# Expert products with the tokens stationary and 512 weight columns (256 gate, 256 up) moving

## What is computed

```python
gate, idx = lax.top_k(aff.T, cap)              # cap = 128 for each expert and group
xe = jnp.take(tok, idx, axis=0)
h = jax.nn.silu(jnp.einsum('ecd,edf->ecf', xe, w_gate)) * jnp.einsum('ecd,edf->ecf', xe, w_up)
ye = jnp.einsum('ecf,efd->ecd', h, w_down) * gate[..., None].astype(x.dtype)
out = jnp.zeros_like(tok).at[idx.reshape(-1)].add(ye.reshape(-1, D))
```

## Time and profile before

| | us |
|---|---|
| Time, median of 3 runs | 3319.93 (3319.58 to 3321.43) |
| Span of the profiled execution, first to last instruction | 3317.6 |
| TensorE busy | 3111.9 (94%) |
| VectorE busy | 1891.1 (57%) |
| ScalarE busy | 1357.6 (41%) |
| GpSimd busy | 477.4 (14%) |

### The profile page before, as it was taken

One profiled execution on the slowest core, in us unless ns is written; L12 is line 12 of the kernel. 1 busy time (PEld: TensorE's weight loads), 2 busy tenths in 40 slices (PEclk: granted clock), 3 DMA queues, 4 the chain that ended last, 5 costly groups with the idle time before them and its releaser, 6 DMA issues.

```text
span 3317.6 us, 54591 instructions
## 1 busy us (share of the span) xinstructions
PE 3111.9 (94%) x21544; PEld 2878.0 (87%) x21544; DVE 1891.1 (57%) x2257; ACT 1357.6 (41%) x1668; POOL 477.4 (14%) x387
## 2 busy tenths in 40 slices
PE   7998999989958999999999999999999999999990
PEld 7997888968848998998989989899898999989990
DVE  6545777856664555555545555555555555555546
ACT  3216777861113334333334343333434333343423
POOL 2543232401120000010010000100010010110005
PEclk9999999999979999999999999999999999999995
DMA  6331101013344566565565655656566565665535
GB/s 203 124 100 49 33 9 30 33 62 121 116 165 133 201 200 204 191 191 202 193 206 190 199 191 191 206 200 197 191 197 203 195 191 198 202 193 202 180 126 215
DMA packets 367271, 533.68 MB, mean 161 GB/s; under 512 B 32592, under 2 KB 307792, under 8 KB 367056
## 3 DMA queue, kind: packets, MB, share of 16 engines
q1 hardware_dynamic: 352464, 488.48, 43.8%
q0 software_dynamic: 10368, 37.75, 4.4%
q10 hardware_dynamic: 4224, 4.19, 0.4%
HBM read 469.57 MB, written 60.82 MB: 160 GB/s over the span
## 4 chain that ended last, share of the span: by engine, by line
issue 66%; PE 18%; DMA 5%; POOLq 4%; POOL 3%; DVE 2%; DVEq 1%; ACT 1%; SPq 0%; ACTq 0%
PE ps_o L747 5%; DMA acc_d<-ysb,idx_s 4%; PE ps_pv L683 4%; PE ps_t L672 3%; PE ps_s L637 2%; PE ps_s L638 2%; POOLq L1585 1%; PE ps_l L764 1%; POOLq L1462 1%; POOLq L1470 1%; POOL qkv L1476 1%; PE ps_m L692 1%; POOLq L1576 1%; POOL w_l L1568 1%; PE ps_m L623 1%
## 5 line engine op out<-in xcount | busy, mean ns | idle before, releaser
L838 PE MATMUL ps_gu<-x_h,w_h 128*128 128x256 f32 x4096 | 1160.5, 283 | 20.0 <-issue 18.5
L838 PE MATMUL ps_gu<-x_h,w_l 128*128 128x256 f32 x4096 | 1159.1, 283 | 0.0
L838 PE MATMUL ps_gu<-x_l,w_h 128*128 128x256 f32 x4096 | 1159.1, 283 | 0.0
L1338 DVE TENSOR_TENSOR w_l<-w_raw,w_h 128x2048 fp32r<-128x2048 f32 x380 | 859.4, 2290 | 288.0 <-ACT w_h L1076 288.0
L838 PEld LDWEIGHTS ps_gu<-x_h,w_h 128*128 128x128 f32 x4096 | 786.3, 192 | 25.8 <-issue 23.9
L1076 ACT ACTIVATE w_h<-w_raw 128x2048 fp32r<-128x2048 f32 x384 | 719.3, 1907 | 195.5 <-PE ps_y L853 186.3
L838 PEld LDWEIGHTS ps_gu<-x_l,w_h 128*128 128x128 f32 x4096 | 786.3, 192 | 0.1
L838 PEld LDWEIGHTS ps_gu<-x_h,w_l 128*128 128x128 f32 x4096 | 786.3, 192 | 0.0
L1101 ACT ACTIVATE sg<-ps_gu 128x256 f32<-128x256 f32 x256 | 98.1, 383 | 941.9 <-PE ps_gu L838 941.9
L1389 DVE TENSOR_TENSOR hf<-sg,ps_gu 128x256 f32<-128x256 f32 x256 | 107.1, 418 | 578.4 <-ACT sg L1101 578.4
L853 PE MATMUL ps_y<-w_h,hh 128*128 128x512 f32 x1024 | 321.5, 395 | 0.0
(11 more groups left out here) (193 smaller groups left out, 3909.6 us busy)
## 6 DMA issues: line engine op xcount, KB each, us to landing
w_raw<-in_w_gate SPq DMA_DIRECT2D x128, 1024.0 KB, 5.3
w_raw<-in_w_up SPq DMA_DIRECT2D x128, 1024.0 KB, 6.1
w_raw<-in_w_down SPq DMA_DIRECT2D x128, 1024.0 KB, 6.0
xin<-in_x SPq DMA_DIRECT2D x16, 512.0 KB, 5.9
xln_d<-xln SPq DMA_DIRECT2D x16, 512.0 KB, 5.5
res<-xln_d SPq DMA_DIRECT2D x16, 512.0 KB, 3.2
h_d<-hid SPq DMA_DIRECT2D x16, 512.0 KB, 2.6
acc_d<-acc SPq DMA_DIRECT2D x16, 512.0 KB, 2.6
```

Of the source, the lines that this page charges most:

```text
L838: last = nc.tensor.matmul(ps_gu[n % 3][:, u, :], w[:, k, cols], a[:, k, :], start=k == 0 and q == 0, stop=k == KD - 1 and q == 2)
L1338: nc.vector.tensor_tensor(w_l[:, c % RING, :], w_raw[:, c % RING, :], w_h[:, c % RING, :].bitcast(f32), ALU.subtract).then_inc(w_lo, 1)
```

## The change

The tokens of one group (128) become the stationary operand of the gate and up products, and the weights move, 512 columns at a time: 256 of gate and the same 256 of up, side by side.

- There are 8 blocks j of 256 hidden columns (`FBLK`). A weight piece is now half of the contraction (4 steps, `KC`) with gate and up columns beside each other, loaded by two DMAs. `landed` gives the count for both.
- A block is two halves, `gate_up(e, j, 0)` and `gate_up(e, j, 1)`; each has 12 products for token group 0 and 12 for group 1. Each group has a bank of its own, `ps_gu[n % 3]` with n = 2j + g. TensorE signals the end of the first half (its weight piece is free) and, in the second half, of each group.
- ScalarE's silu and VectorE's product work on 128 tokens by 256 hidden columns of a group. `hf` now has tokens on the partitions, so TensorE transposes it, four tiles of 128x128 a block, into `ps_x` (`hidden_transposes`): for block j - 1 between the halves of block j, for the last block after down step 0.
- ScalarE copies the four transposed tiles to `hh` in one instruction (`hidden_hi`), VectorE writes `hl` in one (`hidden_lo`) and signals `h_split`.
- ScalarE and VectorE take one weight piece, then the transposed tiles of the block before, then the two groups, then another weight piece. The first x round waits until the transposed tiles have been read out of `ps_x`.

```diff
         def used(e, c):
             if c < NUP:
-                return gu_done, KF * e + 2 * (c // 2) + 2
+                return gu_done, GU * e + 3 * (c // 2) + (3 if c % 2 else 1)
             return dn_done, (KF // 2) * e + (c - NUP) + 1
+
+        def landed(e, c):
+            return W_ROUND * e + 16 * (2 * (c // RING) + 2 if c < NUP else 2 * (NUP // RING) + (c - NUP) // RING + 1)
...
# SyncE
                     if c < NUP:
-                        w = (w_gate, w_up)[c % 2]
-                        src = w[ex, :, (c // 2) * 2 * P:(c // 2 + 1) * 2 * P].rearrange("o (k p) f -> p (o k) f", p=P)
-                        dst = dst.rearrange("p (k f) -> p k f", k=KD)
+                        j, kh = divmod(c, 2)
+                        dst = w_raw[:, c % RING, :].rearrange("p (k u f) -> p k u f", k=KC, u=2)
+                        for u, w in enumerate((w_gate, w_up)):
+                            src = w[ex, kh * KC * P:(kh + 1) * KC * P, j * FB:(j + 1) * FB]
+                            sp.dma_start(dst[:, :, u, :], src.rearrange("o (k p) f -> p (o k) f", p=P)
+                                         ).then_inc(w_dma[c % RING], 16)
...
# TensorE
+            def gate_up(e, j, kh, first):
+                c = 2 * j + kh
+                pe.wait_ge(w_lo, NCHUNK * e + c + 1)
+                wh = w_h[:, c % RING, :].rearrange("p (k f) -> p k f", k=KC)
+                wl = w_l[:, c % RING, :].rearrange("p (k f) -> p k f", k=KC)
+                for g in range(GROUPS):
+                    n = GROUPS * j + g
+                    tok = slice(g * CAP, (g + 1) * CAP)
+                    if kh == 0 and not (first and n < 3):
+                        pe.wait_ge(hf_ready, GROUPS * FBLK * e + n - 2)
+                    out_gu = ps_gu[n % 3][:, :, :].rearrange("p u f -> p (u f)")
+                    for kk in range(KC):
+                        k = kh * KC + kk
+                        for q, (a, w) in enumerate(((x_h, wh), (x_h, wl), (x_l, wh))):
+                            last = nc.tensor.matmul(out_gu, a[:, k, tok], w[:, kk, :],
+                                                    start=k == 0 and q == 0, stop=k == KD - 1 and q == 2)
+                    if kh == 1:
+                        last.then_inc(gu_done, 1)
+                if kh == 0:
+                    last.then_inc(gu_done, 1)
+
+            def hidden_transposes(e, j):
+                pe.wait_ge(hf_ready, GROUPS * (FBLK * e + j) + 2)
+                if j:
+                    pe.wait_ge(h_split, FBLK * e + j)
+                for sub in range(2):
+                    for g in range(GROUPS):
+                        last = nc.tensor.transpose(ps_x[:, GROUPS * sub + g, :], hf[:, j % 2, g, sub * P:(sub + 1) * P],
+                                                   ident[:, :])
+                last.then_inc(hx_done, 1)
...
-                for n in range(KF):
...
+                for j in range(FBLK):
+                    gate_up(e, j, 0, first)
+                    if j:
+                        hidden_transposes(e, j - 1)
+                    gate_up(e, j, 1, first)
...
                     last.then_inc(dn_done, 1)
+                    if m == 0:
+                        hidden_transposes(e, FBLK - 1)
...
# ScalarE
+                for j in range(FBLK):
+                    w_hi_copy(e, 2 * j + RING, False)
+                    if j:
+                        hidden_hi(j - 1)
+                    for g in range(GROUPS):
+                        n = GROUPS * j + g
+                        act.wait_ge(gu_done, GU * e + 3 * j + 2 + g)
+                        if not (first and n < 2):
+                            act.wait_ge(hf_ready, GROUPS * FBLK * e + n - 1)
+                        nc.scalar.activation(sg[:, g, :], ps_gu[n % 3][:, 0, :], ACT.Silu).then_inc(silu_done, 1)
+                    w_hi_copy(e, 2 * j + 1 + RING, False)
...
# VectorE
-                        nc.vector.tensor_tensor(hf[:, n % 2, :], sg[:, n % 2, :], ps_gu[n % 3][:, 1, :], ALU.mult)
-                        dve.drain()
-                        nc.vector.tensor_copy(hh[:, n, :], hf[:, n % 2, :])
-                        dve.drain()
-                        nc.vector.tensor_tensor(hl[:, n, :], hf[:, n % 2, :], hh[:, n, :].bitcast(f32),
-                                                ALU.subtract).then_inc(h_split, 1)
...
+                for j in range(FBLK):
+                    w_lo_sub(e, 2 * j + RING)
+                    if j:
+                        hidden_lo(j - 1)
+                    for g in range(GROUPS):
+                        n = GROUPS * j + g
+                        dve.wait_ge(silu_done, GROUPS * FBLK * e + n + 1)
+                        if g == 0 and not (first and j < 2):
+                            dve.wait_ge(hx_done, FBLK * e + j - 1)
+                        nc.vector.tensor_tensor(hf[:, j % 2, g, :], sg[:, g, :], ps_gu[n % 3][:, 1, :],
+                                                ALU.mult).then_inc(hf_ready, 1)
+                    w_lo_sub(e, 2 * j + 1 + RING)
```

More of the change, by code:

```diff
@@ L216, in encoder_layer @@
         ysb = sb("ysb", [P, GROUPS, D])
-        sg = sb("sg", [P, 2, C2])
-        hf = sb("hf", [P, 2, C2])
+        FB = 2 * P
+        sg = sb("sg", [P, GROUPS, FB])
+        hf = sb("hf", [P, 2, GROUPS, FB])
         lmax = sb("lmax", [P, TILES])
@@ L240, in encoder_layer @@
         idx_s = sb("idx_s", [P, GROUPS], u32)
-        ps_gu = [pb(f"ps_gu{i}", [P, 2, C2]) for i in range(3)]
+        ps_gu = [pb(f"ps_gu{i}", [P, 2, FB]) for i in range(3)]
         ps_y = [pb(f"ps_y{i}", [P, D]) for i in range(GROUPS)]
@@ L251, in encoder_layer @@
         xt_d, x_hi, x_lo = sem("xt_d"), sem("x_hi"), sem("x_lo")
-        gu_done, silu_done, h_split = sem("gu_done"), sem("silu_done"), sem("h_split")
+        gu_done, silu_done, hf_ready = sem("gu_done"), sem("silu_done"), sem("hf_ready")
+        hx_done, h_hi, h_split = sem("hx_done"), sem("h_hi"), sem("h_split")
         dn_done, y_ready = sem("dn_done"), sem("y_ready")
@@ L272, in encoder_layer @@
         y_st = [sem(f"y_st{i}") for i in range(FR)]
-        NCHUNK = 2 * KF // 2 + KF // 2
-        NUP = KF
+        FBLK = F // FB
+        KC = KD // 2
+        NUP = 2 * FBLK
+        NCHUNK = NUP + KF // 2
+        GU = 3 * FBLK
+        W_ROUND = 16 * (2 * NUP + KF // 2) // RING
         def x_bank(n, start):
@@ L514, in stage_e @@
                         sp.wait_ge(w_lo, NCHUNK * e + c - RING + 1)
-                    dst = w_raw[:, c % RING, :]
                     if c < NUP:
-                        w = (w_gate, w_up)[c % 2]
-                        src = w[ex, :, (c // 2) * 2 * P:(c // 2 + 1) * 2 * P].rearrange("o (k p) f -> p (o k) f", p=P)
-                        dst = dst.rearrange("p (k f) -> p k f", k=KD)
+                        j, kh = divmod(c, 2)
[4 more added lines that the diff above has]
+                                         ).then_inc(w_dma[c % RING], 16)
                     else:
@@ L522, in stage_e @@
                         src = w_down[ex, m * 2 * P:(m + 1) * 2 * P, :].rearrange("o (k p) d -> p (o k) d", p=P)
-                        dst = dst.rearrange("p (k d) -> p k d", k=2)
-                    sp.dma_start(dst, src).then_inc(w_dma[c % RING], 16)
+                        dst = w_raw[:, c % RING, :].rearrange("p (k d) -> p k d", k=2)
+                        sp.dma_start(dst, src).then_inc(w_dma[c % RING], 16)
             steps(sp, E, stage_e)
@@ L814, in x_round @@
                     pe.wait_ge(x_lo, XR * e + n)
+                    if n == 0:
+                        pe.wait_ge(h_split, FBLK * e)
                 dst = x_bank(n, start)
@@ L843, in stage_e @@
                     pe.wait_ge(w_lo, NCHUNK * e + c + 1)
-                    pe.wait_ge(h_split, KF * e + 2 * m + 2)
+                    pe.wait_ge(h_split, FBLK * e + m + 1)
                     if m == 0 and not first:
@@ L1072, in w_hi_copy @@
             def w_hi_copy(e, c, start):
-                act.wait_ge(w_dma[c % RING], 16 * ((NCHUNK // RING) * e + c // RING + 1))
+                act.wait_ge(w_dma[c % RING], landed(e, c))
                 if not start:
@@ L1095, in stage_e, with hidden_hi @@
             def stage_e(e, first, last_e):
-                for j in range(KF // 2):
-                    for n in (2 * j, 2 * j + 1):
-                        act.wait_ge(gu_done, KF * e + n + 1)
+                def hidden_hi(j):
+                    act.wait_ge(hx_done, FBLK * e + j + 1)
+                    if j == 0 and not first:
+                        act.wait_ge(dn_done, (KF // 2) * e)
+                    nc.scalar.activation(hh[:, 2 * j:2 * j + 2, :].rearrange("p k t -> p (k t)"),
+                                         ps_x[:, :, :].rearrange("p c t -> p (c t)"), ACT.Copy).then_inc(h_hi, 1)
+                for j in range(FBLK):
[5 more added lines that the diff above has]
+                        act.wait_ge(gu_done, GU * e + 3 * j + 2 + g)
                         if not (first and n < 2):
```

(23 more changed lines are left out.)

## The result

The changed kernel takes **3279.39 us** (3278.12 to 3280.51, 4 runs), the kernel before, run again beside it, 3320.68: a ratio of 0.987, interval 0.9858 to 0.9881. It is 41 us faster, and the forecast was 20.5. The direction was right, the time (3299.4) and the range (3284 to 3312) were not.

What follows compares the result with a forecast made beforehand. TensorE's instruction stream was taken to bound the expert stage. Per block -0.64 us for wider products and +0.48 for transposes, over 128 blocks, gave -20.5 us: 3299.4 us from a median of 3319.93, range 3284 to 3312.

Steps and rivals of the forecast that it cites:

- TensorE's stream sets the stage: Expert stage: it is as long as TensorE's instruction stream, busy 138.15 of 139.47 us; only a shorter stream shortens it.
- 512-column products at 0.2267 us, a group at 0.48, a block at -0.16: Gate/up blocks: wider products save 0.64 us, four added transposes cost 0.48; 128 blocks give -20.5 us.
- Weight pieces and the new chain between engines for nothing: Expert stage: 16 more DMA issues an expert and new waits between engines cost nothing, within 3.3 us of slack or more.
- Unchanged. The loop's turns: the row itself is the price, nothing in the change touches what follows a branch: TensorE's expert loop: its 13 turns keep costing 1.75 us each; if they halved, 11 us less.
- only columns count: Gate/up products: 512 columns cost two of 256, 0.240 us, so transposes add 61 us, 3381; chance 0.02.
- The group empties TensorE: Transposes in mid-block: four run one after another, 1.10 us instead of 0.48, +59 us, 3379; chance 0.06.
- The break lingers: The 24 products behind each transpose group run at 0.2325 us, nearly all gain gone, 3317; chance 0.06.
- Faster still: Products behind the transposes are not set back, a group costs 0.36 us: 15 us more gain, 3284; chance 0.10.

Runs made afterwards that it cites:

- The straight stream: Kernel before with TensorE's loop over experts written out straight, 16 experts and no branch: 3299.91 us, ratio 0.9935 to the kernel before.
- the two runs with 256 columns: Changed kernel with 512-column products made as two of 256: in gate and up 3375.36 us, in the down products 3381 us (single run).
- the run with each group done twice: Changed kernel with each group of four transposes of the hidden values done twice into the same place: 3334.82 us.
- the narrow down products: Changed kernel with down products of 256 columns: 3381 us (single run); with 48 more instructions ahead of the loop, moving its body: 3321.41 us.
- the run with `n >= 14`: Kernel before with the x_l product (remainder of the tokens) of gate and up left out in blocks 14 and 15: 3325 us, single run.

## Why the prediction was wrong, and where it was right

- *TensorE's stream sets the stage*: right. In every run the time followed TensorE's intervals and gaps, and none of its waits in the loop was for another engine.
- *512-column products at 0.2267 us, a group at 0.48, a block at -0.16*: right. The block came at 11.36 us; the kernel before without turns is 20.5 us slower than the changed one, 1.27 us an expert. A second group behind a first costs 0.43.
- *Weight pieces and the new chain between engines for nothing*: right. No wait of TensorE for hf, a bank or a piece appears.
- *"Unchanged. The loop's turns: the row itself is the price, nothing in the change touches what follows a branch"*: **this is the step that failed.** The branch did not change, but the amount of code that it goes back over did: the body went from 8 code blocks to 6, and 13 x 1.75 = 22.8 us went with the reloading. The straight stream, which has no turns, measured this term alone: 3321.19 us for the kernel before, run beside it, against 3299.91, 21.3 us. The prediction saw that TensorE's idle time was "issue", waiting for nothing shown, and took it as a constant instead of asking what is loaded there. The queue of kind instruction was on the page, and a change that takes a third of the instructions out of a loop should have raised the question. The range then left out the end at which the turns are free: 3299.4 - 22.8 = 3277, 3 us from the result.
- *The rivals*: "only columns count" is excluded by the two runs with 256 columns (+0.59 a block, +0.31 a down step), and with it, for these streams, the 2.5 ns that the Trainium skill ("TensorE: Matmul & The Clock Gate", Back-to-back issue gap) gives for a product by itself, by which the change would have lost: the fixed part is 13 ns. "The group empties TensorE" is excluded by the block of 11.36 us, which would be 11.98 at 1.10 us a group, and by the missing wait for hf; the run with each group done twice could not tell, since its second group waits for nothing. "The break lingers": the first product behind a group takes 0.32 us and some ten after it 0.23, but that is inside the 0.48. "Faster still" named the right side, with the wrong cause.

## What to carry to other kernels

Idle time called "issue" at the turns of a loop was code being loaded here: look at the packets of the instruction queue inside the loop, and count the loop's instructions on that engine before and after a change. A body on TensorE that stayed was worth a gap a turn, and just above the limit 48 instructions ahead of the loop, which moved its start, were worth 60 us, more than the change itself. Wider moving operands save the fixed part of each product, here 13 ns of 120, as long as what they cost (here transposes of 0.48 us a block against 0.64) is counted from intervals and not from records.

## What was not expected of the hardware

A branch to code that isn't at hand cost 1.5 to 1.75 us where the loop began well ahead of a code block's end, and 4.8 to 6.8 us where it began 18 to 24 instructions ahead of one: 143.5 - 138.7 us an expert with the narrow down products, and 140.5 against 133.7 in the run with `n >= 14`, first passes without a turn taken as the base. Behind the second stop of the latter, 3.3 us without a product, the granted clock was 0.52; behind that of the former, 1.51 us at the turn shown, it was 1.00 from 2015.68 to 2018.00 us. Straight code of the same work, in the run without turns, was loaded ahead and showed no gap at all.
